# Weaving the second block of tokens 0-255 with the expert gather of tokens 256-511

## What is computed

```python
a = gelu(einsum('td,ted->te', hb, u_tab[eb]))      # 128 dots per token
w = gates * a
out = einsum('te,ted->td', w, v_tab[eb])
x = x + gate2 * out                                # then final_g norm
```

## Time and profile before

| what | us |
|---|---|
| median of 3 runs (2965.42 to 2969.78) | 2968.13 |
| the profiled execution | 2965.35 |
| its span, first to last instruction | 2963.6 |
| TensorE's mean granted clock, share of full speed | 0.871 |
| PE / DVE / ACT / POOL busy, share of the span | 78% / 44% / 25% / 36% |

### The profile page before, as it was taken

The page is one execution under the profiler, slowest core; times in us unless marked ns, Lnnn a source line. Parts: engine busy times, 40 slices in busy tenths (PEclk is TensorE's granted clock), DMA queues, the critical chain, the costliest instruction groups (busy, mean ns, idle before and its releaser), DMA issues. The chain is left out here.

```text
span 2963.6 us, 22217 instructions
## 1 busy us (share of the span) xinstructions
PE 2303.9 (78%) x7379; PEld 1329.2 (45%) x7379; DVE 1289.2 (44%) x2945; ACT 744.4 (25%) x1626; POOL 1071.8 (36%) x746
## 2 busy tenths in 40 slices
PE   4896698681677777777786877776967997778899
PEld 1345343571233333333332333332746885556787
DVE  1107541317667666775668555554252102243101
ACT  1202231211111111111111111112444444344443
POOL 1000000220434444444443444442704885400687
PEclk8897698895898999989998999987958998866999
DMA  6100151323999999999999999995603664300465
GB/s 214 51 14 0 57 171 57 94 74 127 420 420 420 409 420 420 420 385 419 421 419 416 398 420 420 420 420 230 212 0 99 186 185 141 107 1 8 144 185 161
DMA packets 172295, 710.32 MB, mean 240 GB/s; under 512 B 18033, under 2 KB 70812, under 8 KB 106140
## 3 DMA queue, kind: packets, MB, share of 16 engines
q0 software_dynamic: 73728, 536.90, 43.8%
q1 hardware_dynamic: 90576, 168.18, 18.0%
q10 hardware_dynamic: 7886, 3.93, 0.5%
HBM read 699.24 MB, written 9.72 MB: 239 GB/s over the span
## 5 line engine op out<-in xcount | busy, mean ns | idle before, releaser
L1382 PE MATMUL ps<-uv_ring,expert_diag 128*128 128x512 f32 x2048 | 1008.1, 650 | 340.4 <-ACT expert_diag L1351 340.3
L1187 POOL DMA_INDIRECT uv_ring<-in_peer_uv_dram,expert_idx x512 | 556.2, 1086 | 821.5 <-PE ps L1382 712.5
L1306 DVE CUSTOM_DVE_ANT_0 uv_ring<-uv_ring,h_rows 128x1024 f32<-128x1024 f32 x512 | 628.9, 1230 | 492.0 <-DMA uv_ring<-in_peer_uv_dram,expert_idx 491.4
L1382 PEld LDWEIGHTS ps<-uv_ring,expert_diag 128*128 128x128 f32 x2048 | 414.4, 208 | 933.5 <-issue 500.3
L1464 POOL TENSOR_TENSOR w_low_b<-w_raw_b,w_high_b 128x1024 fp32r<-128x1024 f32 x98 | 234.4, 2394 | 262.6 <-ACT w_high_b L1458 261.2
L1351 ACT ACTIVATE expert_diag<-ident,expert_weight 128x128 f32<-128x128 f32 x512 | 163.6, 390 | 623.5 <-DVE expert_weight L1278 623.5
L1464 POOL TENSOR_TENSOR w_low_a<-w_raw_a,w_high_a 128x1024 fp32r<-128x1024 f32 x98 | 235.2, 2403 | 199.4 <-ACT w_high_a L1458 198.1
L271 POOL TENSOR_TENSOR peerq_low<-peerq_raw,peerq_high 128x1024 fp32r<-128x1024 f32 x16 | 38.1, 2381 | 550.6 <-ACT peerq_high L260 550.6
L1344 ACT ACTIVATE expert_gelu<-expert_dot 128x4 f32<-128x4 f32 x128 | 26.3, 205 | 495.7 <-DVE expert_dot L1306 495.7
L1458 ACT CAST w_high_b<-w_raw_b 128x1024 fp32r<-128x1024 f32 x98 | 102.9, 1053 | 116.8 <-PE ps L1477 116.8
L1458 ACT CAST w_high_a<-w_raw_a 128x1024 fp32r<-128x1024 f32 x98 | 102.9, 1052 | 115.4 <-PE ps L1477 115.4
(11 more groups left out here) (399 smaller groups left out, 2896.2 us busy)
## 6 DMA issues: line engine op xcount, KB each, us to landing
w_raw_a<-in_w_gu_dram SPq DMA_DIRECT2D x44, 512.0 KB, 3.5
w_raw_b<-in_w_gu_dram SPq DMA_DIRECT2D x44, 512.0 KB, 3.6
wada_rest<-in_w_ada_dram SPq DMA_DIRECT2D x16, 1024.0 KB, 5.3
w_raw_a<-in_w_in_dram SPq DMA_DIRECT2D x24, 512.0 KB, 4.4
w_raw_b<-in_w_in_dram SPq DMA_DIRECT2D x24, 512.0 KB, 4.0
w_raw_a<-in_w_down_dram SPq DMA_DIRECT2D x22, 512.0 KB, 3.6
w_raw_b<-in_w_down_dram SPq DMA_DIRECT2D x22, 512.0 KB, 3.5
wada<-in_w_ada_dram SPq DMA_DIRECT2D x4, 2048.0 KB, 8.5
```

What stands on the lines that cost most here:

```text
L1187: pool.indirect_dma_start(out=ring[:, n % RING, :], out_offset=None, in_=K.uv, in_offset=bass.IndirectOffsetOnAxis(ap=idx[tb % 2][:, s:s + ...
L1306: dve.tensor_tensor_reduce(u, u, hN[:, tb, :], 1.0, 0.0, ALU.mult, ALU.add, a[tb % 2][:, s:s + 1]).then_inc(s_dot, 1)
L1382: last = nc.tensor.matmul(K.ps[2 * (tb % 2) + half][:, :], diag[n % DIAGS][:, :], ring[:, n % RING, D + 512 * half:D + 512 * half + 512], ...
```

## The change

The gather runs in two phases. A first stage gathers for tokens 0-255 alone (256 slots, ring of 12). Then `stage_half` for tokens 0-255 contains a `Gather` of tokens 256-511 (256 slots), whose instructions are woven into every engine's list. The last stage is the second half alone, as before. `Gather` places slot n at `us * n`, with `us` = 2.5 in the first phase and `plan.us / 256` in the woven one; there the ring has 6 buffers. Groups are of 2 slots, with 4 diagonals, and one pair of PSUM banks (6, 7) for all blocks. Routing works on 4 heads at a time, so that a block's first 64 indices are ready ahead of the others; the first phase also routes block 2 ahead.

- h and x go through DRAM as rows: 64 transposes in `stage_peer_scores` with 16 copies and 16 stores issued by ACT; `Gather` loads h, then x, and stores the updated x; `stage_half` loads x.
- The rows of the bias table are built in the first phase (`BiasRows`, the DVE copies and the DMA of the former `Bias`).
- Woven, the weights have 3 raw and 2 split buffers, differential attention has one pair of score banks in place of two, `Ffn` one pair of banks for gate and up in place of two.
- `diff_us` and `stick_us` are 6.0 and 3.2 for the woven half.
- Silu becomes a Tanh on ACT and one more DVE operation, in both halves.
- Keys of the two halves are two tensors, so a score product of the second half is two matmuls.

```diff
 class Weights:
-    KK, RAW, SPLIT, LEAD = 2, 4, 3, 2
+    KK = 2
...
+        self.RAW, self.SPLIT, self.LEAD = raw, split, split - 1
...
 # stage_peer_scores, tensor
+            for n, (src, _, b, half) in enumerate(ROWS):
+                if n >= 4:
+                    pe.wait_ge(s_rc[n % 2], (n - 4) // 2 + 1)
+                for k in range(4):
+                    last = nc.tensor.transpose(K.ps[4 + n % 4][:, k * P:(k + 1) * P],
+                                               src[:, 4 * half + k, b * P:(b + 1) * P], K.ident[:, :])
+                last.then_inc(s_rt, 1)
             pe.wait_ge(h.s_lo, KD)
 # stage_peer_scores, scalar (vector copies the odd n)
             h.high(act)
+            for n, (_, dst, b, half) in enumerate(ROWS):
+                if n % 2 == 0:
+                    act.wait_ge(s_rt, n + 1)
+                    if n >= 4:
+                        act.wait_ge(s_rs[n % 4], 16 * (n // 4))
+                    act.copy(rows[n % 4][:, :], K.ps[4 + n % 4][:, :]).then_inc(s_rc[0], 1)
+                act.wait_ge(s_rc[n % 2], n // 2 + 1)
+                act.dma_start(dst[b, :, 512 * half:512 * half + 512], rows[n % 4][:, :]).then_inc(s_rs[n % 4], 16)
             pr.highs(act, PEER_H, 0)
...
+class Gather:
+    G, DIAGS, HG = 2, 4, 4
...
+    def at(self, n):
+        return self.start + self.us * n
...
+    def pool(self, pool):
+        for n in range(self.n):
+            b, s = divmod(n, SLOTS)
+            yield self.at(n - self.RING + 2.5)
+            if s % 64 == 0:
+                i = 2 * (b - (1 if self.routed else 0)) + s // 64 + 1
+                if i > 0:
+                    pool.wait_ge(self.s_idx, i)
+            if n == self.RING - 1:
+                pool.wait_ge(self.s_gr, 1)
+            if n >= self.RING:
+                pool.wait_ge(self.s_pv, n - self.RING + 1)
+            pool.indirect_dma_start(
...
+    # dve: dot of slot n at place at(n); the weighing of a group behind the dot of the next slot
+            if n % G == 0 and n:
+                yield place + 0.1 * self.us
+                weigh(n // G - 1)
+            if s == 1 and b:
+                yield place + 0.5 * self.us
+                update(b - 1)
...
+    # act
+        for g in range(self.n // G):
+            yield self.at(G * g + 1.1)
+            act.wait_ge(self.s_dot, G * (g + 1))
+            act.activation(self.gl[b % 2][:, c], self.a[b % 2][:, c], ACT.Gelu).then_inc(self.s_gelu, 1)
+            yield self.at(G * g + 2.2)
+            act.wait_ge(self.s_w, g + 1)
+            for j in range(G):   # diagonals
...
+    # pe
+            yield self.at(n - n % self.G + 2.3 + 0.1 * (n % self.G))
+            if s == 0 and b:
+                pe.wait_ge(self.s_y, 4 * b)
+            pe.wait_ge(self.s_diag, n + 1)
...
+        g = Gather(K, ctx, experts, True, None, 0.0, 1.0, (6, 7), 6) if experts else None
+        W, plan = Weights(K, ctx, 3 if g else 4, 2 if g else 3), Plan()
...
+        if g:
+            g.us = plan.us / g.n
...
         def _(pe):
-            weave(in_turn(t1.pe(pe, [(n1.s_un, nb)]), p2.pe(pe), diff.pe(pe), stick.pe(pe), t2.pe(pe, stick.done()),
+            weave(*([g.pe(pe)] if g else []),
+                  in_turn(t1.pe(pe, [(n1.s_un, nb)]), p2.pe(pe), diff.pe(pe), stick.pe(pe), t2.pe(pe, stick.done()),
...
+    stage_gather(K, [0, 1], 2)
+    K.recycle()
+    K.tag = "_a"
+    first = Half(K, ctx, 0, 2, None, 6.0, 3.2)
+    stage_half(K, first, [2, 3])
+    K.recycle()
+    K.tag = "_b"
+    stage_half(K, Half(K, ctx, 2, 2, first, 4.0, 1.6), None)
```

In `Ffn`:

```diff
-                    act.activation(self.silu[b][:, :], self.bank(g, b)[:, 0:256], ACT.Silu).then_inc(self.s_silu, 1)
+                    act.activation(self.silu[b][:, :], self.bank(g, b)[:, 0:256], ACT.Tanh, scale=0.5).then_inc(self.s_silu, 1)
...
-                    dve.tensor_tensor(self.prod[b][:, :], self.silu[b][:, :], self.bank(g, b)[:, 256:512],
-                                      ALU.mult).then_inc(self.s_prod, 1)
+                    dve.scalar_tensor_tensor(out=self.silu[b][:, :], in0=self.silu[b][:, :], scalar=1.0,
+                                             in1=self.bank(g, b)[:, 0:256], op0=ALU.add, op1=ALU.mult).then_inc(self.s_gated, 1)
+                    dve.wait_ge(self.s_gated, g * self.nb + b + 1)
+                    dve.scalar_tensor_tensor(out=self.prod[b][:, :], in0=self.silu[b][:, :], scalar=0.5,
+                                             in1=self.bank(g, b)[:, 256:512], op0=ALU.mult, op1=ALU.mult).then_inc(self.s_prod, 1)
```

More of the change, by code:

```diff
@@ new lines, in stage_gather, with _ @@
+def stage_gather(K, blocks, ahead):
+    nc = K.nc
+    with ExitStack() as ctx:
+        g = Gather(K, ctx, blocks, False, ahead, 0.0, 2.5, (6, 7), 12)
+        bias = BiasRows(K, ctx, 100.0)
+        block = ctx.enter_context(nc.Block())
+        @block.sync
+        def _(sp):
+            weave(g.sp(sp), g.rows(sp), bias.sp(sp))
+        @block.gpsimd
+        def _(pool):
+            weave(g.pool(pool))
+        @block.vector
+        def _(dve):
+            weave(g.dve(dve), bias.dve(dve))
+        @block.scalar
+        def _(act):
+            weave(g.act(act))
+        @block.tensor
+        def _(pe):
+            weave(g.pe(pe))
@@ L1664, in act @@
                 elif n >= 4:
[L1665 to L1666 removed]
+                    dst = (self.half.dvx, self.half.svx)[n - 4]
+                    act.copy(dst[:, b, :], self.bank(n, b)).then_inc(self.s_val, 1)
             if n < 2:
@@ L2287, in stage_half @@
-        p2 = In2(K, W, plan, half, t1)
-        diff = Diff(K, plan, half, p2.done(), (bias.s_bm, 1) if bias else p2.done()[0],
-                    {"s": (0, 1, 2, 3), "t": (4, 5), "o": (6, 7)})
-        stick = Stick(K, plan, half, diff.done(), {"z": (0, 1), "r": (2, 3), "o": (4, 5)})
-        scratch.close()
+        with ExitStack() as K.phase:
+            p2 = In2(K, W, plan, half, t1, [un[:, i, :].rearrange("p (a b) -> p a b", a=2) for i in range(2)])
+        with ExitStack() as K.phase:
+            diff = Diff(K, plan, half, p2.done(), (half.s_bm, 1),
+                        {"s": (0, 1), "t": (2, 3), "o": (4, 5)} if g else {"s": (0, 1, 2, 3), "t": (4, 5), "o": (6, 7)})
@@ L2292, in stage_half @@
+        with ExitStack() as K.phase:
+            stick = Stick(K, plan, half, diff.done(), {"z": (0, 1), "r": (2, 3), "o": (4, 5)})
         K.phase = ctx
         at = plan.take([5.0])
-        t2 = Turn(K, "mix", [half.mix[:, b, :] for b in range(nb)], split, [K.ps[j][:, :] for j in range(4)],
+        t2 = Turn(K, "mix", [half.mix[:, b, :] for b in range(nb)], split, four,
                   [K.diffw[:, 0:1]] * 4 + [K.vecT[:, V_SBN:V_SBN + 1]] * 4, at[0])
-        o2 = Out2(K, W, plan, half, t2, (6, 7, 4, 5))
+        o2 = Out2(K, W, plan, half, t2, (4, 5, 0, 1))
```

681 lines of the change are left out of this document (338 added, 343 removed).

## The result

The changed kernel takes **3123.94 us** in the median of 4 runs (3119.34 to 3129.44), the kernel before 2966.78 in 4 runs beside it: 1.053 times, 95% interval 1.051 to 1.055. The forecast was 2877 us, faster; it is wrong in sign, and the time lies above the range. The profiled execution took 3122.9 us, its span is 3121.2.

What follows compares the result with a forecast made beforehand. DMA was taken to bound the gather, PE and chains between engines the second block. First phase 1386 + woven phase 985 + second half 501 = 2872; with time around the span 2874, median 2877 us; range 2750 to 3015.

Steps and rivals of the forecast that it cites:

- Scores stage, +13: Scores stage: transposes, copies and 16 stores issued by ACT come ahead of the first product, unhidden; +13 us, bounds 5 and 25.
- Start of the gather, -24: First gather: with 4 heads ready POOL issues 26 us earlier, less 2 for the first freed buffer; bounds 15 and 27.
- The first phase's rate, 2.5 us: Unwoven gather of 256 slots: rate unchanged at 2.5 us per slot, set by DMA; last dot at 1370, phase end 1386.
- Stick ... I take 8.3 per step, 175: Woven Stick: 21 steps through PE, ACT and DVE, ACT 4.5 to 7.1 us each; taken as 8.3, in all 175 us.
- rival 2: Woven Diff and Stick become a serial chain, 12.4 us per Stick step, 260; woven phase 1094, total 2986; chance 0.24.
- Ffn 112 x 3.7 = 415: Woven Ffn: 112 slots at 3.7 us each, limited by the short ring, 415 us.
- norm 25: Second norm of the woven half: 7 slots at 3.6 us, 25 us.
- The chain of 6 buffers: Woven ring: buffer freed, issue, landing, dot, PE, 11.6 us for 4 slots; 2.9 per slot bare, 3.6 to 3.7 in stages.
- Start 30: First norm of the woven half: 8 slots, with the load of x first, 30 us.
- In2 152, Diff 112, Out2 66, drain 10, second half 501: Times in us for three woven stages, the woven phase's drain and store, and the unwoven second half with its load of x.
- Rival 3: Woven phase: DVE's dots and POOL's 98 subtractions cannot overlap; +59 us, total 2936; chance 0.10.
- The woven phase as such: Gather of tokens 256-511 woven with the first half of the second block: 985 us, against 1055 for the same work before.

Runs made afterwards that it cites:

- the gelu's table: Changed kernel with the woven gather's gelu replaced by a copy, so ACT need not change its table between gather and attention: 3093.42 us.
- without the low part: Changed kernel with POOL's subtraction for the split weights replaced by a memset of 0: 3072.15 us.
- the fastest version: Changed kernel with Stick free of slots, Ffn's ACT and DVE places later and seven woven ring buffers: 2902.91 us, ratio 0.9811 to the kernel before.

## Why the prediction was wrong, by its own steps

- **Scores stage, +13:** measured +15 (scores stored at 674.1 instead of 659.1). Right.
- **Start of the gather, -24:** this step failed. The first issue came 10.7 us earlier than before (724.88 against 735.57; some 13 were forecast), but the first dot came at 755.45 instead of 743.07, as DVE routed the other four heads until 754. POOL filled 11 buffers by 739 and then stood 16.6 us:

```profile
738.23 0.93 POOL L1268 DMA_INDIRECT uv_ring_g<-in_peer_uv_dram,expert_idx  x1 [0.30 <-issue]
755.80 1.67 POOL L1268 DMA_INDIRECT uv_ring_g<-in_peer_uv_dram,expert_idx  x1 [16.64 <-DVE gate_rows_g L1388]
```

  "DMA stays busy until DVE starts" held, but the first freed buffer came dearer than the 2 us taken off for it: POOL's next issue into one is at 764.55, 9 us behind the first dot, and DMA lost 7.5 us in 20 (windows of 5 us, columns as in the earlier trace rows):

```profile
750.00:755.00 5.00, 0.00 (x0) 0.00 (x0) 4.38 (x10) 1.59 (x2) 0.00 (x0) 0.50 1.01 419
755.00:760.00 5.00, 0.00 (x0) 0.00 (x0) 5.00 (x14) 0.20 (x1) 1.67 (x1) 0.50 0.74 256
760.00:765.00 5.00, 4.51 (x6) 1.93 (x7) 5.00 (x16) 1.80 (x6) 0.45 (x1) 0.50 0.26 110
765.00:770.00 5.00, 5.00 (x12) 2.25 (x11) 5.00 (x17) 1.30 (x4) 3.42 (x3) 0.88 0.54 182
770.00:775.00 5.00, 5.00 (x13) 2.15 (x12) 5.00 (x18) 1.39 (x5) 3.17 (x3) 1.00 0.96 352
```

- **The first phase's rate, 2.5 us:** too low as well. From first dot to last it comes out as (1394.4 - 755.5) / 255 = 2.5, but some eleven slots had been transferred before the first dot. From 725 to 1395 the queues moved (packets, MB, share of 16 engines)

```profile
q0 software_dynamic: 36864, 268.45, 96.9%
q1 hardware_dynamic: 1392, 4.46, 1.7%
```

  and the 4.46 MB of scores, bias rows, h and x are 10.6 us at 420 GB/s, a term that the forecast put at nothing. Its own rows already had 2.53 per slot: (2036.67 - 743.07) / 511. Together 2.3 (first issue), 5.5 (freed buffer) and 10.6 are 18 of the 24 us by which the last dot was late (1394.4 instead of 1370); 6 are open. The drain took 12.6 us instead of 16, so the phase ended at 1407 instead of 1386. Groups of 2 and one pair of banks cost nothing: DMA's share is 1.01 from 777 to 1372.
- **"Stick ... I take 8.3 per step, 175":** the step that decided. Measured 242, 11.5 per planned step of 21 (16 of them have scores). I went from ACT's busy time in a step (4.5 to 7.1) to 8.3, while rival 2 added up the way round PE, ACT, DVE, ACT and PE again, 12.4, and came to 260. The way round is what the timeline shows. Three table loads a step with scores and the gelu's own came true (64 in Stick, 81 in Diff and Stick; 110 expected), at the row's price: load at 1843.61, next operation at 1844.91. The Trainium skill's 2.66 with a drain (ScalarE: Activation LUTs, What ACT_TABLE_LOAD costs) is not borne out here either. Slots taken out of Stick gave 107 us, the gelu's table without them 47.
- **"Ffn 112 x 3.7 = 415", "norm 25":** measured 514 together, against 440. The chain of 6 buffers was the wrong mechanism there, although its price per slot was near: the ring with 7 gave 5 us, later places of Ffn's operations on ACT and DVE gave 72. I priced Ffn's buffers and its extra operation and not these places. With a gather pair in front of PE's turn, DVE stood at ffn_low for 9.6 us in the mean of 11 groups, 11.2 at most, with landed slots behind it.
- **Start 30:** 66. ACT waited 37.9 us for x and DVE 26.6 for the gate rows. The forecast had "the load of x first", but POOL had three gathers out when x was issued and five soon after, and x took 23 us from its issue. With the gathers held back it took 11, and the first dot in front of the norm took up most of the difference.
- **In2 152, Diff 112, Out2 66, drain 10, second half 501:** 166, 121, 84, 16, 505, near but each above, 51 together. In In2 the port is up to 11 of the 14 (166 to 155 without the low part); the causes of the others are open.
- **Rival 2** (2986, chance 0.24) had the sign, the place and nearly the size in Stick (260; measured 242) and in Diff (17 per step; measured 121 / 8 = 15). It stayed 137 us too low because it was summed with the forecast's other terms.
- **Rival 3**, the port, is real, +52 at most (it said +59); it came beside rival 2 and not in its place. That the rivals were taken as alternatives, where they add up, is why the upper end of 3015 was too low: first phase and start (57), Stick (67), Ffn with its norm (74) and the rest (51) make the 249.
- **The woven phase as such** could be had: with Stick free, Ffn's places moved and 7 buffers it took 970 us to the last addition, where the forecast had 975 up to there. That it meets the sum says nothing for the forecast's terms, since this kernel has other places and another ring. What keeps it above 2877 is mainly the part before it (1410 instead of 1386).

## What to carry to other kernels

When two streams are merged into in-order engines, price a step by walking once round through every engine that it passes, with what stands in front at each, and not by the busiest engine's share; then compare the price of an item there with its price alone (here 5.1 against 2.5 us) and leave the items out of the stages where it is dearer. Look for engines that wait for something unrelated while their woven work is ready. A deeper ring pays only once no list holds finished items up: 12 us before those repairs, 55 after.

## What the runs showed of the hardware

A dot (two operands in SBUF) beside a subtraction on POOL takes up to 4.1 us instead of 1.2; 256 of them took 368 us instead of 313 in the first phase. The timeline of after has a pair side by side:

```profile
2313.11 3.31 POOL L1559 TENSOR_TENSOR w_low_a<-w_raw_a,w_high_a 128x1024 fp32r<-128x1024 f32 x1 [3.81 <-ACT w_high_a L1553]
...
2314.14 3.36 DVE L1400 CUSTOM_DVE_ANT_0 uv_ring_a<-uv_ring_a,h_rows_a 128x1024 f32<-128x1024 f32 x1
```

With POOL only writing, no dot of the woven gather was longer than 1.26 us. The Trainium skill (SBUF — State Buffer, Who interferes with whom) says just this, that such a DVE instruction contends with a GpSimd one that reads SBUF and not with one that only writes; these runs agree. The denser the weave, the dearer it gets: a dot has 1704 ns in the mean in the fastest version, hidden there under DMA.

TensorE's granted clock follows the weave: 0.72 in Stick, 0.92 in Ffn, 1.00 in Ffn once its order was mended. A gap can thus cost more than its length: in the step above, 8 matmuls behind 7.5 idle us took 5.61 us instead of 3.6.

ACT loaded its table three times per step of Exp, Ln and Exp once a gelu had come between (14, 16 and 16 loads in 16 steps), although one load had served all of them in the kernel before; each load took 1283 ns.
